# A two-block network in split fp32 on one core: four taps of a convolution on TensorE, a streamed norm, and 512-column matmuls in four projections

## The reference, cut to what matters

```python
# first block
h = x * (1.0 + sc1) + sh1                      # sh, sc, g: six vectors from silu(c) @ w_ada + b_ada
z_u, z_v, z_h, z_g = split(h @ w_in + b_in)    # 1024, 1024, 3072, 4096 columns
y_a = spatial_gating(gelu(z_u), gelu(z_v), ...) @ w_branch_a
y_b = hyena(z_h, ...) @ w_branch_b             # begins with a short convolution of 3 taps over z_h
gate_a, gate_b = split(sigmoid(z_g))
x = layer_norm(ALPHA * x + g1 * ((gate_a * y_a + gate_b * y_b) @ w_o + b_o))
f = square(relu((x * (1 + sc2) + sh2) @ w_m1 + b_m1)) @ w_m2 + b_m2     # feed-forward, width 8192
x = layer_norm(ALPHA * x + g2 * f)
# second block, layer 0
a, b, z = split(rms_norm(x) @ conv_w_in, 3)                  # 2048 columns each
v = depthwise_conv(a * sigmoid(b), 31 taps) + dw_b           # along the tokens
x = x + (silu(layer_norm(v)) * silu(z)) @ conv_w_out
# second block, layer 1
q, a_f, a_b, i, z = split(rms_norm(x) @ hgrn_w_in, 5)        # 16 heads of 128
log_f = logaddexp(log(lb), log1p(-lb) + log_sigmoid(a));  key = (1 - lb) * sigmoid(-a)
o = rms_norm(scan(q, k_f, i, log_f) + reversed_scan(...))    # per head, with chunk-wise scores
x = x + (o * silu(z)) @ hgrn_w_out
```

## Time and profile before

| what | us |
|---|---|
| median of three runs | 2782.59 |
| profiled execution | 2780.93 |
| its span | 2779.1 |
| busy: PE | 2582.7 (93%) |
| busy: DVE | 2018.7 (73%) |
| busy: ACT | 1401.7 (50%) |
| busy: POOL | 840.3 (30%) |
| mean granted clock of TensorE, as a share of full | 0.967 |

### The profile page before, as it was taken

The page is one execution under the profiler, slowest core; times in us unless marked ns, Lnnn a source line. Parts: engine busy times, 40 slices in busy tenths (PEclk is TensorE's granted clock), DMA queues, the critical chain, the costliest instruction groups (busy, mean ns, idle before and its releaser), DMA issues.

```text
span 2779.1 us, 46348 instructions
## 1 busy us (share of the span) xinstructions
PE 2582.7 (93%) x18408; PEld 2430.1 (87%) x18408; DVE 2018.7 (73%) x2576; ACT 1401.7 (50%) x2108; POOL 840.3 (30%) x780
## 2 busy tenths in 40 slices
PE   4599998999997999999999979997799999999989
PEld 1489998999996888888888879987699999999979
DVE  7888765767867876555555568887657899999964
ACT  0154323344435543444544456666556777777753
POOL 0100000001214621001101058888102666666630
PEclk9799999999998999999999989999899999999989
DMA  9978754787873877665566535554355444444434
GB/s 320 340 257 268 231 200 156 239 267 242 270 246 116 291 258 227 190 189 183 190 194 189 185 101 167 167 159 128 102 171 158 150 152 152 150 147 149 148 105 146
DMA packets 146353, 534.84 MB, mean 192 GB/s; under 512 B 16631, under 2 KB 16792, under 8 KB 145688
## 3 DMA queue, kind: packets, MB, share of 16 engines
q1 hardware_dynamic: 143176, 520.33, 58.2%
q0 software_dynamic: 2960, 11.54, 1.2%
HBM read 525.51 MB, written 6.29 MB: 191 GB/s over the span
## 4 chain that ended last, share of the span: by engine, by line
PE 58%; DVE 16%; issue 7%; POOL 7%; ACT 6%; DMA 5%; SPq 0%; POOLq 0%; DVEq 0%; ACTq 0%
PE ps L541 13%; PE ps L528 11%; PE ps L530 10%; PE ps L529 10%; PE ps L543 7%; DVE wl L942 5%; POOL misc L2200 5%; DMA ring<-in_w_ada 4%; ACT wh L1640 2%; DVE AF L961 1%; PE ps L581 1%; DVE BF L1527 1%; PE ps L663 1%; PE ps L651 1%; DVE BF L1517 1%
## 5 line engine op out<-in xcount | busy, mean ns | idle before, releaser
L942 DVE TENSOR_TENSOR wl<-ring,wh 128x1024 fp32r<-128x1024 f32 x784 | 1031.4, 1328 | 381.7 <-ACT wh L1640 380.8
L528 PE MATMUL ps<-A,wh 128*128 128x256 f32 x3424 | 997.2, 291 | 17.0 <-DVE wl L942 10.4
L1640 ACT CAST wh<-ring 128x1024 fp32r<-128x1024 f32 x784 | 814.8, 1043 | 381.5 <-PE ps L530 212.2
L529 PE MATMUL ps<-A,wh 128*128 128x256 f32 x3424 | 974.4, 285 | 0.0
L530 PE MATMUL ps<-A,wl 128*128 128x256 f32 x3424 | 974.3, 285 | 0.0
L528 PEld LDWEIGHTS ps<-A,wh 128*128 128x128 f32 x3424 | 663.1, 194 | 21.8 <-issue 10.8
L529 PEld LDWEIGHTS ps<-A,wh 128*128 128x128 f32 x3424 | 663.3, 194 | 1.2
L530 PEld LDWEIGHTS ps<-A,wl 128*128 128x128 f32 x3424 | 662.2, 193 | 0.0
L541 PE MATMUL ps<-B,wh 128*128 128x512 f32 x1024 | 357.9, 394 | 0.0
L541 PE MATMUL ps<-A,wh 128*128 128x512 f32 x960 | 337.5, 396 | 2.2 <-DVE wl L942 2.2
L543 PE MATMUL ps<-B,wl 128*128 128x256 f32 x1024 | 287.3, 281 | 0.0
(11 more groups left out here) (247 smaller groups left out, 3323.3 us busy)
## 6 DMA issues: line engine op xcount, KB each, us to landing
ring<-in_w_m SPq DMA_DIRECT2D x256, 512.0 KB, 4.5
ring<-in_hgrn_w_in SPq DMA_DIRECT2D x160, 512.0 KB, 3.8
ring<-in_w_ada SPq DMA_DIRECT2D x144, 512.0 KB, 6.6
ring<-in_w_in SPq DMA_DIRECT2D x144, 512.0 KB, 4.9
ring<-in_conv_w_in SPq DMA_DIRECT2D x96, 512.0 KB, 3.9
AF<-in_w_ada SPq DMA_DIRECT2D x48, 512.0 KB, 9.1
ring<-in_w_ab SPq DMA_DIRECT2D x32, 512.0 KB, 5.2
ring<-in_w_o SPq DMA_DIRECT2D x32, 512.0 KB, 5.4
```

Of the source, the lines that this page charges most:

```text
L528: e.matmul(dst, hi[:, k, :], xh, start=first and k == 0, stop=False)
L529: e.matmul(dst, hi[:, k, :], xl, start=False, stop=False)
L942: e.tensor_tensor(low[:], ring[SLOT[h]][:], hi[:].bitcast(F32), ALU.subtract).then_inc(s.lo, 1)
L1640: e.copy(wh[h % NSPLIT][:], ring[SLOT[h]][:]).then_inc(s.hi, 1)
```

## The change

What it does, part by part:

1. `wide_half` and `half` become one (`k_tile` picks the form by the width of the destination). w_in, w_o, conv_w_out and hgrn_w_out now get a full bank: one matmul of 512 columns and one of 256 for each k-tile. conv_w_in, hgrn_w_in and w_ab keep three of 256. ACT evicts columns 256 to 511 with the bias, and DVE adds columns 0 to 255. In w_in the nonlinearity (Gelu, Sigmoid) is then a second ACT operation from SBUF, one block later.
2. In the convolution, 4 of the 31 taps go to PE, as matmuls with diagonal matrices that ACT makes (`diag`); DVE has 15, ACT with POOL 12. The order `N_CV` spreads ten z blocks over the tiles and leaves six at the end. The z silu is one ACT operation.
3. The norm of the convolution is streamed: after eight tiles their mean is taken as a shift, every tile is centred on it and its squares are summed while the stream runs. `normed` and `gated` of all 16 tiles now stand behind the last half of conv_w_in; POOL does half of the products with z. The first two blocks of conv_w_out run k-tile by k-tile together (`two_halves`). Sixteen POOL operations (`scale_rows`) move from the norm ahead of conv_w_in into its ticks 8 to 23.
4. In each HGRN head DVE loses four operations (the affine step and the maximum go into scale and bias of two ACT Ln; the tables are limited once ahead) and the reciprocal (ACT does Ln and Exp with scale -0.5 in place of Sqrt). ACT's order within a tick puts the steps by kind. A head has 24 steps in place of 22.
5. The DMA of `k_window` signals the semaphore of `hy_w3`, so that PE's filter matmuls wait for both.

```diff
+        def k_tile(dst, hi, lo, x, first, last):
+            if dst.shape[1] == 512:
+                e.matmul(dst.rearrange("p (a t) -> p a t", a=2), hi, x, start=first, stop=False)
+            else:
+                e.matmul(dst, hi, x[:, 0, :], start=first, stop=False)
+                e.matmul(dst, hi, x[:, 1, :], start=False, stop=False)
+            return e.matmul(dst[:, 0:256], lo, x[:, 0, :], start=False, stop=last)
...
         for i, n in enumerate(N_IN):
-            pb = bank()[:, 0:256]
+            pb = bank()[:]
...
+        def add_halves(i, dst, pb):
+            w.wait_ge(s.ev, i + 1)
+            return e.tensor_tensor(dst, dst, pb[:, 0:256], ALU.add)
...
             if i < 24:
+                add_halves(i, pad[i % 2][:, 1:257], pb).then_inc(s.zin, 1)
                 short_conv(i, pad[i % 2], zh(i))
+            else:
+                add_halves(i, in_tile(n), pb).then_inc(s.pre, 1)
...
-NPOOL = 15
+NPOOL = 12
+NPE = 4
...
-for _i in range(NTRIPLE):
-    N_CV += [16 + _i, _i, 32 + _i]
-for _i in range(NTRIPLE, 16):
+for _i in range(16):
     N_CV += [16 + _i, _i]
-N_CV += list(range(32 + NTRIPLE, 48))
+    if NZ * (_i + 1) // 16 > NZ * _i // 16:
+        N_CV.append(32 + NZ * _i // 16)
+N_CV += list(range(32 + NZ, 48))
...
+        def conv_step(n, step):
+            if step == 1:
+                w.wait_ge(s.cpad, n + 1)
+                w.wait_ge(s.diag, NPE * (n + 1))
+                w.wait_ge(s.dt, n)
+                w.wait_ge(s.hv, 48)
+                for i in range(NPE):
+                    j = NDVE + NPOOL + i
+                    done = e.matmul(pe_taps, diag[i], cpadb[n % 2][:, j:j + 256], start=i == 0, stop=i == NPE - 1)
+                done.then_inc(s.pt, 1)
...
+        w.wait_ge(s.rc, 5)
+        for i in range(16):
+            normed(i)
+
+        def add_out(n, pb):
+            own.up(e.tensor_tensor(XR[:, n, :], XR[:, n, :], pb[:, 256:512], ALU.add))
+            w.wait_ge(s.own, own.n)
+            e.tensor_tensor(XR[:, n, :], XR[:, n, :], pb[:, 0:256], ALU.add).then_inc(s.xr, 1)
...
-                    for k in range(2):
-                        lb = lbtab[:, 32 * k + hd:32 * k + hd + 1]
-                        om = lbtab[:, 32 * k + 16 + hd:32 * k + 17 + hd]
-                        x = sig[0][:, 256 * k:256 * k + 256]
-                        own.up(e.tensor_scalar(x, x, om, lb, ALU.mult, ALU.add))
-                        w.wait_ge(s.own, own.n)
-                        e.tensor_scalar(slot(u, 6 + k), x, 2.0 ** -64, None, ALU.max).then_inc((s.f2, s.f3)[u], 1)
...
+            for k in range(2):
+                e.activation(slot(u, 6 + k), sig[0][:, 256 * k:256 * k + 256], ACT.Ln,
+                             scale=lbtab[:, 32 * k + 16 + hd:32 * k + 17 + hd],
+                             bias=lbtab[:, 32 * k + hd:32 * k + hd + 1]).then_inc((s.ln0, s.ln1)[u], 1)
...
-            e.reciprocal(ost[u], ost[u]).then_inc(s.orc, 1)
-            w.wait_ge(s.orc, hd + 1)
```

More of the change, by code:

```diff
@@ L339, in _build @@
     odd_taps = [ps[3 + i][:, 256:512] for i in range(2)]
+    pe_taps = ps[5][:, 0:256]
+    diag = [misc[:, 5184 + P * i:5184 + P * i + P] for i in range(NPE)]
+    first_mean_sb = rstd
+    left_sq, left_var = tmpA[0], tmpA[1]
     pacc = [misc[:, 3136 + 256 * i:3392 + 256 * i] for i in range(2)]
@@ L526, in half, with two_halves @@
                 ready(k)
[L527 to L530 removed]
+                done = k_tile(dst, hi[:, k, :], lo[:, k, :], tiles(k), first and k == 0, last and k == 7)
                 if k == 7:
                     done.then_inc(s.mm, 1)
[L535 to L547 removed]
+        def two_halves(h, first, second, ready, begin, end, behind=lambda k: None, xs=lambda k: A2[:, :, k, :]):
             for j in range(2):
@@ L915, in tensor_program @@
                     heads_behind(x)
-        early = [bank()[:, 0:256] for n in range(NEARLY)]
+        early = [bank()[:] for n in range(NEARLY)]
         done_heads = lambda k: w.wait_ge(s.blo, 85 + k + 1)
@@ L1948, in conv_behind @@
-            if 9 <= c < 13:
-                for i in range(4 * c - 36, 4 * c - 32):
-                    gated(i)
+                if step < 6:
+                    tap_step(n, step)
+                square_step(n, step)
+            g, odd = divmod(tick - LAST_TILE - 1, 2)
+            if 0 <= 4 * g < NZ and not odd:
+                n = min(NZ, 4 * g + 4) - 4 * g
+                zs = BF[:, 16 + 4 * g:16 + 4 * g + n, :]
+                w.wait_ge(s.scl, scaled[32 + 4 * g + n - 1])
+                e.activation(zs, zs, ACT.Silu).then_inc(s.sgz, 1)
@@ L1952, in scalar_program @@
+            if tick == LAST_TILE + 12:
+                w.wait_ge(s.mean, 4 + 16)
+                w.wait_ge(s.cpad, 16)
+                e.activation(left_sq[:], mean_ap, ACT.Square).then_inc(s.dd, 1)
+                w.wait_ge(s.va, 3)
+                w.wait_ge(s.sub, 26)
+                e.activation(rstd, left_var[:], ACT.Sqrt, bias=sm[:, 1:2]).then_inc(s.sd, 1)
         for i, n in enumerate(N_CV):
-            pb = bank()[:, 0:256]
+            bank()
             for part in range(2):
@@ L2235, in head @@
                 yield
-            for _ in range(5):
+            for _ in range(6):
                 yield
```

375 lines of the change are left out of this document (203 added, 172 removed).

## The result

The changed kernel takes 2760.17 us (median of four runs, 2757.61 to 2767.32) where the kernel before takes 2785.27 (four runs). The ratio is 0.9914, with a 95% interval of 0.9898 to 0.9931: 25 us or 0.9% faster, clear of noise, but little more than half of the 43 us forecast, and 2 us outside the range. The profiled execution took 2759.44 us.

A forecast was written before the change was run, and what follows sets the result against it. Four engines take turns as the bound: PE in w_in and the feed-forward, a DVE, ACT and POOL chain in conv_w_in. Terms summing to -43.4 took 2780.93 to 2737.5, at the level of the median 2739; range 2722 to 2758 us.

The forecast's parts named there:

- w_in and w_o, -13.7 forecast: Wide matmuls in two projections: -12.5 us in w_in (bounds -5 and -15.1), -1.2 in w_o (0 to -3.4).
- that is 0.015, with rounding 0.013 to 0.015; I take 0.013: In w_in, the wide form's saving in us per k-tile, 0.36 against 0.345; 15.1 us for 72 blocks.
- That DVE would just keep up in the first 24 blocks: In w_in, DVE's wait of 0.78 us a block covers the added operation, 0.42, and shorter period, 0.21, leaving 0.15.
- conv_w_in, -11.8 with its norm: conv_w_in -11.3 us (0 to -19), 314 instead of 325.6; the norm ahead of it -0.5 (0 to -1.5).
- I leave 8 us of waits: In conv_w_in, waits added to PE's content of 306 us, giving 314, since PE and DVE are both near full.
- The slow rival: In conv_w_in, taps make PE wait at L821 for cpad, 62 us over 16 tiles: 2812 us; chance 0.05.
- The norm and conv_w_out's start: From conv_w_in's end to the second conv_w_out block's eviction: 27 us instead of 29.5, -2.5, bounds 22 and 33.
- 16 to 20 us in which PE works along: Behind conv_w_in, DVE and POOL normalise 16 tiles while PE does two conv_w_out blocks (11.1 us) k-tile by k-tile.
- HGRN, -10.5 forecast: In hgrn_w_in, DVE's relief gives 0.7 us a head over 15 heads; bounds -5 and -19.
- The preamble, +1.0 forecast: Before w_in, the filter matmuls wait for one more DMA: +1.0 us (0 to +1.5).
- hgrn_w_out, -2.9 forecast: Thirteen blocks and the early ones give -3.4 us; the last block's second addition costs +0.46 at the end.
- the wide matmul saves little here: Rival: a wide k-tile costs nearly what three narrow ones do; 1920 give 5 us, not 20: 2757 to 2759; chance 0.06.

The follow-up runs named there:

- an expectation above: Expectation for 2 taps on PE and 14 on ACT and POOL, against the changed kernel's 4 and 12, pricing a tap matmul at 0.408 us; measured 2765.65 us.

## Why the prediction was wrong

Its sum was -43.4, the profiled executions differ by 21.5 us. No single step accounts for that; four failed by 5 to 7 us each. By its own steps:

*w_in and w_o, -13.7 forecast, -6.9 measured.* The step "that is 0.015, with rounding 0.013 to 0.015; I take 0.013" failed. It took the wide form's price from one place, and that place was in the quick phase. The trace of before held the slow phase too, 0.3534 from 893 to 975 us, which I had not looked for; in it the saving is 0.0067. In the changed profile the wide k-tiles of these stages stood at least 5.8 us in all above 0.3467 (summed over the recorded starts). Of the 18.8 that 88 blocks give in the quick phase that leaves 13; PE's waits rose by 3.5 us (27.5 to 31.0 in all), and about 1 us more went to k-tiles at the lower clock, which leaves 8.5, 1.6 more than measured. By parts, w_in gained 10.1 where 12.5 was put. w_ab, for which the sum had no term, lost 1.2 to waits. w_o lost 2.0 where 1.2 of gain was put: 1.4 us more of waits, and behind its chunk's group at 806.7 us k-tiles began 0.64 us apart, with 0.52 of the clock granted from 808.9 to 811.5, where the kernel before stayed at 0.36. That DVE would just keep up in the first 24 blocks was right: the wait for ACT fell from the 15.3 of the earlier trace rows to 5.3, and the first sixteen blocks, in the quick phase, gained 0.20 us each where 0.21 was forecast.

*The feed-forward, no term, +4.9 measured.* The unnamed step was that untouched code keeps its time. It takes 751.1 to 765.1 us over the eleven comparable profiles with the alternating order; its 2048 k-tiles at 0.0067 would be 13.7 if all changed phase, and up to 1560 of them (10 us) did. Of the 4.9 here some 2.6 are 392 more k-tiles in the slow phase, and 2.9 are longer waits (3.14 against 1.10 us at one group of one-column matmuls).

*conv_w_in, -11.8 with its norm, -16.8 measured.* The mechanism was right, and so nearly was PE's content: from the third block's first matmul to the last k-tile it took 307.6 us without a wait, where 306 of content and 314 in all were forecast (325.3 before). "I leave 8 us of waits" was too cautious. The working for the stage before was off by little as well: PE waited 30.0 us there, not 33, and a tap costs 0.43 us, not 0.42. Two small slips stand in its sums: 314 for 325.6 is -11.6, not -11.3, and 1979.3 to 2009.05 is 29.75 us, not 29.5. The slow rival didn't come: L821 never waited, although it stands only two halves behind its tile.

*The norm and conv_w_out's start, -2.5 forecast, +2.6 measured, and +3.5 from the end of the last k-tile on (29.7 to 33.2, past the upper bound of 33).* "16 to 20 us in which PE works along" failed: it did so for the first halves of both blocks only and then stood 8.94 us. I had counted the activations and not the weights of the fourth half, which the order of both engines puts behind them. Undoing that gave 6.3 us, and with it the stretch took the 27 of the forecast.

*HGRN, -10.5 forecast.* The loop was the right one. Its first part measured 8.72 us (2270.85 to 2279.57) where I took 8.5, and the second 26.59 where 25.48 + 0.9 = 26.4 was taken: 0.26 a head instead of 0.7, since a small difference of large terms carries every error of theirs. Over all fifteen distances the mean fell by 0.33 (35.24 to 34.91), and the whole stage by 5.2 us, with the wait ahead of hgrn_w_out in it. That ACT's chain would set the pace was in the sum; what I did not see is that the cast at its end, for which DVE stood idle 3.4 us, could go ahead of it. In the kernel before, the same move gave nothing (35.62).

*The preamble, +1.0 forecast, +3.1 measured,* and 4.3 against the same kernel with its own semaphore. *hgrn_w_out, -2.9 forecast, -1.7 measured.* The wait ahead of it, put at -0.5, grew from 5.36 to 6.53; it counts in the row of HGRN. The stage took 113.4 to 116.1 us over all profiles with wide k-tiles in it, so the 1.2 us that it gave less lie within its scatter.

Of the rivals, "the wide matmul saves little here" came nearest (2757 to 2759, given 0.06), for another reason than the one that it named. The Trainium skill, in "TensorE: Matmul & The Clock Gate", section "Back-to-back issue gap", adds that in a real stream both the weight load and the matmul set the spacing; that the order of long and short matmuls changes the rate (0.3483 in pairs) agrees with it. The 325 ns that its rule for isolated ones gives for a 512 and a 256, an estimate, stays below all three rates measured.

What stays open is what chooses the phase. It changes at interruptions, and one kind foretold it (behind a single 256-column sum with no wait after it the quick phase came, 25 times of 25), but the count of others did not, and the clock was at its full level in both.

## What to carry to other kernels

When an engine is relieved, look at once at what it waits for next: here the relief of DVE gave 0.3 us a head, and moving one cast ahead of two table loads gave 1.0 more. When a serial stretch is put between two stages, list the weights of the next stage too, and place those whose buffers are already free inside it. Take the price of a streaming instruction as a mean over long stretches from several places of the trace, not from one pair of rows: two rates 2% apart, set anew at each interruption, and the waits beside them moved one stage of this kernel by up to 14 us with the same code. And before an effect is called chance, look whether it failed at the places where its condition held: the sum of 256 columns failed only where PE waited behind it.

## What the hardware showed that I had not expected

A stream of alternating 512- and 256-column fp32r matmuls ran at 0.3467 or at 0.3534 us for the two, stable until other matmuls or a wait broke in. In the order 512, 512, 256, 256 it ran at 0.3483 everywhere, and three matmuls of 256 at 0.3600. Four fp32 tap matmuls of 256 columns cost 1.73 us, 0.43 each (the low matmuls of the k-tiles on either side start 2.09 us apart instead of 0.36), close to the 0.42 taken from the row sums; the 0.408 in an expectation above is too low.
